# Latents normed in the input projection, latent products in split halves, and two gate units moved to the S5 stage

## The reference, cut to what matters

```python
proj = h @ w_in
c_q, c_kv, k_r, fq, fk, fv, f_logit, u, gate_logits = jnp.split(proj, split_points, axis=-1)
q  = einsum('bsr,rhd->bshd', rms_norm(c_q, q_lat_norm_g), w_uq)      # 384 -> 4 heads x 96
kv = einsum('bsr,rhd->bshd', rms_norm(c_kv, kv_lat_norm_g), w_ukv)   # 256 -> 4 heads x 128
k_nope, v_mla = kv[..., :64], kv[..., 64:]
k_mla = concatenate([k_nope, k_rope], -1)       # k_rope = k_r for each head
q_mla = apply_rope_tail(rms_norm(q, mla_q_norm_g), cos, sin)
k_mla = apply_rope_tail(rms_norm(k_mla, mla_k_norm_g), cos, sin)
o_mla = causal_block_attention(q_mla, k_mla, v_mla)
...
gates = sigmoid(gate_logits.reshape(bsz, seq, 3, 1024))
merged = einsum('bsnd,bsnd->bsd', gates, projected)
```

## Time and profile before

| | |
|---|---|
| median of 3 runs | 1647.36 us (1645.93 to 1648.49) |
| profiled execution, its own time | 1651.23 us |
| its span, first to last instruction | 1649.4 us |
| TensorE busy | 1521.9 us, 92% |
| VectorE busy | 939.9 us, 57% |
| ScalarE busy | 621.7 us, 38% |
| GpSimd busy | 126.6 us, 8% |
| mean granted TensorE clock | 0.967 |

### The profile page before, as it was taken

One profiled execution on the slowest core, in us unless ns is written; L12 is line 12 of the kernel. 1 busy time (PEld: TensorE's weight loads), 2 busy tenths in 40 slices (PEclk: granted clock), 3 DMA queues, 4 the chain that ended last, 5 costly groups with the idle time before them and its releaser, 6 DMA issues. The chain is left out here.

```text
span 1649.4 us, 19066 instructions
## 1 busy us (share of the span) xinstructions
PE 1521.9 (92%) x7214; PEld 1265.8 (77%) x7214; DVE 939.9 (57%) x1290; ACT 621.7 (38%) x1013; POOL 126.6 (8%) x104
## 2 busy tenths in 40 slices
PE   5999999987997988787899978999999999999999
PEld 4899877776576777676678767888888888888887
DVE  4310345666285665674783557887778887433333
ACT  4310224541222554212452335555555555332322
POOL 1000150002033000310120100000000000000000
PEclk9899999997998999898999989999999999999999
DMA  5130131103022000313455112322222221644643
GB/s 193 44 121 1 47 94 34 38 27 130 19 83 66 31 26 26 90 48 113 156 190 215 54 39 64 102 77 90 77 77 90 90 77 68 212 148 145 245 143 138
DMA packets 126500, 153.65 MB, mean 93 GB/s; under 512 B 11530, under 2 KB 94397, under 8 KB 126141
## 3 DMA queue, kind: packets, MB, share of 16 engines
q1 hardware_dynamic: 126224, 152.40, 28.3%
q10 hardware_dynamic: 189, 0.08, 0.0%
HBM read 115.55 MB, written 36.31 MB: 92 GB/s over the span
## 5 line engine op out<-in xcount | busy, mean ns | idle before, releaser
L486 PE MATMUL ps<-split_arena 128*128 128x512 f32 x1152 | 298.9, 414 | 25.3 <-ACT plain_arena L521 8.6
L1715 PE MATMUL ps<-split_arena 128*128 128x512 f32 x1320 | 308.0, 390 | 4.7 <-DVE split_arena L2253 3.5
L1715 PEld LDWEIGHTS ps<-split_arena 128*128 128x128 f32 x1320 | 247.8, 188 | 57.2 <-DVE split_arena L2253 4.0
L486 PEld LDWEIGHTS ps<-split_arena 128*128 128x128 f32 x1152 | 221.9, 198 | 74.1 <-issue 21.3
L1805 PE MATMUL ps<-down_w,down_a 128*128 128x512 f32 x352 | 137.3, 390 | 0.7 <-DVE down_w L1782 0.7
L1807 PE MATMUL ps<-down_w,down_a 128*128 128x512 f32 x352 | 137.1, 390 | 0.0
L1806 PE MATMUL ps<-down_w,down_a 128*128 128x512 f32 x352 | 137.1, 390 | 0.0
L1778 DVE TENSOR_TENSOR down_a<-plain_arena,down_a 128x1024 fp32r<-128x1024 f32 x44 | 53.9, 1225 | 144.5 <-ACT down_a L1767 144.5
L1715 PE MATMUL ps<-up_b,split_arena 128*128 128x512 f32 x528 | 130.7, 398 | 5.0 <-DVE split_arena L1643 4.9
L1715 PEld LDWEIGHTS ps<-up_b,split_arena 128*128 128x128 f32 x528 | 101.7, 193 | 27.1 <-DVE split_arena L1643 5.2
L1767 ACT ACTIVATE down_a<-plain_arena 128x1024 fp32r<-128x1024 f32 x44 | 46.7, 1061 | 161.6 <-PE ps L1807 146.5
(11 more groups left out here) (333 smaller groups left out, 2495.5 us busy)
## 6 DMA issues: line engine op xcount, KB each, us to landing
plain_arena<-scr_act SPq DMA_DIRECT2D x44, 512.0 KB, 3.6
plain_arena<-in_w_in SPq DMA_DIRECT2D x24, 512.0 KB, 4.2
scr_gate<-plain_arena SPq DMA_DIRECT2D x48, 256.0 KB, 2.0
plain_arena<-scr_gate SPq DMA_DIRECT2D x24, 512.0 KB, 4.6
plain_arena<-in_w_up SPq DMA_DIRECT2D x22, 512.0 KB, 5.1
up_raw<-in_w_up SPq DMA_DIRECT2D x22, 512.0 KB, 5.1
scr_act<-plain_arena SPq DMA_DIRECT2D x22, 512.0 KB, 2.6
plain_arena<-in_w_down SPq DMA_DIRECT2D x44, 256.0 KB, 3.9
```

The lines of the kernel that those rows point to most:

```text
L486: mm = nc.tensor.matmul(m.ps[:, self.banks[half], :], w[:, k, :], src[:, k, h * BANK:(h + 1) * BANK], start=(j == 0), stop=(j == self.PER_ ...
L1715: mm = nc.tensor.matmul(o, self.w[j][w][:, k, :], self.h[j][k][h], start=(j in self.OPENS and k == 0 and n == 0), stop=(k == self.HK - 1 a ...
```

## The change

It has six parts.

1. **Input projection.** ScalarE squares and sums the latents row tile by row tile (`lat_squares`, two row tiles behind the copies of chunk 1), VectorE makes the means, GpSimd the powers, VectorE scales the latents in place during chunk 3. The spill to memory waits for that.
2. **Latent transposes.** They need no norm any more and stand behind one gate unit instead of two. Each fill is split: ScalarE writes the high half with the gain, VectorE the low half. The two weights are split too, by ScalarE behind the sixth fill and by VectorE behind the eighth. Half a gate unit stands between the transposes and the products.
3. **Products.** Three fp32r matmuls each in place of one float32 matmul.
4. **Preparation of q and k.** ScalarE copies k's part; VectorE does square, sum and mean of k and of q first, then the low halves of v, then the rest. GpSimd's order is two splits of gate weights, the two powers, and then all other splits.
5. **The queue.** The 35 loads for S5 stand behind the units of the preparation; the semaphores of the stages before are cleared in the MLA stage, ahead of its last unit.
6. **Gate units.** 4, 1, 4, 4, 3 in place of 4, 2, 5, 3, 2: two units move from the MLA stage to the S5 stage, one to each of its groups.

Several buffers move within the core's memory; the squares of the preparation lie in another arena.

```diff
# stage_load_norm_project
-            sp.wait_ge(out_act, copied(2 * TT - 2))
-            sp.wait_ge(out_dve, copied(2 * TT - 1))
+            sp.wait_ge(lat_normed, 2 * TT)
             sp.dma_start(m.scr_lat, m.lat.rearrange("p a b -> p (a b)")).then_inc(spill, 16)
...
+            m.pool_step(nc.gpsimd.memset(lat_expo, -0.5))
+            pool.wait_ge(lat_ms, 2 * TT)
+            nc.gpsimd.tensor_tensor(lat_rstd, lat_ssq, lat_expo, ALU.pow).then_inc(lat_rstd_done, 1)
...
+            def lat_squares(t):
+                act.wait_ge((out_act, out_dve)[t % 2], copied(TT + t))
+                for i, (a, b) in enumerate(lat_parts):
...
+                    nc.scalar.activation(cols(m.R, 30720, b - a), m.lat[:, t, a:b], ACT.Square,
+                                         accum_out=lat_ssq[:, i * TT + t:i * TT + t + 1]).then_inc(lat_sq, 1)
...
+                if 0 <= n - TT - 2 < TT:
+                    lat_squares(n - TT - 2)
...
+                if n == 2 * TT + 3:
+                    dve.wait_ge(lat_sq, 2 * TT)
...
+                if 0 <= n - 2 * TT - 5 < 4:
+                    dve.wait_ge(lat_rstd_done, 1)
...
-FOX_PREP, MLA_FIRST, MLA_PREP, S5_FIRST, S5_SECOND = 4, 2, 5, 3, 2
+FOX_PREP, MLA_FIRST, MLA_PREP, S5_FIRST, S5_SECOND = 4, 1, 4, 4, 3
# stage_mla, SyncE
+            fill.sync(sp, MLA_FIRST + MLA_PREP)
             for i, v in enumerate((m.ins["s5_lambda_re"], m.ins["s5_lambda_im"])):
...
-            fill.sync(sp, MLA_UNITS)
+            fill.sync(sp, H - 1)
+            for x in past:
+                sp.sem_clear(x)
+            fill.sync(sp, 1)
# GpSimd
-            fill.gpsimd(pool, 1)
-            for n, (a, b) in enumerate(((0, 16), (16, 48), (16, 48))):
+            fill.gpsimd(pool, 2)
+            for n in range(2):
                 pool.wait_ge(ms_done, n + 1)
...
+            fill.gpsimd(pool, MLA_UNITS - 2)
# ScalarE
             for f in range(10):
                 act.wait_ge(filled, f + 1)
...
+                if f == 5:
+                    act.wait_ge(w_in, 48)
+                    for hi, raw in zip(w_hi, w_raw):
+                        nc.scalar.activation(hi, raw, ACT.Copy).then_inc(w_hi_done, 1)
+            fill.scalar(act, UNIT // 2)
...
+            nc.scalar.activation(k[:, :, :, 0:NOPE], kv[:, :, :, 0:NOPE], ACT.Copy).then_inc(k_out, 1)
# TensorE
-            fill.tensor(pe, UNIT)
+            fill.tensor(pe, MLA_FIRST * UNIT)
...
-            fill.tensor(pe, (MLA_FIRST - 1) * UNIT)
-            pe.wait_ge(scaled, 2)
+            pe.wait_ge(lat_in, 16)
+            for f in range(10):
+                r, half = divmod(f, 2)
+                if f >= 4:
+                    pe.wait_ge(lat_lo_done, f - 3)
...
+            fill.tensor(pe, UNIT // 2)
+            pe.wait_ge(lat_lo_done, 10)
+            pe.wait_ge(w_lo_done, 3)
+            def product(o, r, w, row, t, first, last):
+                cut = slice(t * P, (t + 1) * P)
+                for n, (x, y) in enumerate(((lat_hi[:, r, cut], w_hi[w]), (lat_hi[:, r, cut], w_lo[w]), (lat_lo[r][:, cut], w_hi[w]))):
+                    mm = nc.tensor.matmul(o, x, y[:, row, :], start=(first and n == 0), stop=(last and n == 2))
...
-            fill.tensor(pe, MLA_PREP * UNIT)
+            fill.tensor(pe, MLA_PREP * UNIT - UNIT // 2)
# VectorE
+            for f in range(10):
+                dve.wait_ge(lat_hi_done, f + 1)
+                V.scalar_tensor_tensor(out=lat_lo[f // 2][:, lat_cut(f)], in0=m.ps[:, f % 4, :], scalar=lat_gain(f),
...
+                if f == 7:
+                    for i in range(3):
+                        dve.wait_ge(w_hi_done, i + 1)
+                        V.tensor_tensor(w_lo[i], w_raw[i], f32(w_hi[i]), ALU.subtract).then_inc(w_lo_done, 1)
...
+            for n in range(2):
+                step(V.tensor_tensor(sq, flat[n], flat[n], ALU.mult))
+                step(V.tensor_reduce(ssq[n], sq, AX.X, ALU.add))
+                V.tensor_scalar(ssq[n], ssq[n], 1.0 / QK, EPS, ALU.mult, ALU.add).then_inc(ms_done, 1)
             for h in range(H):
                 dve.wait_ge(v_hi, h + 1)
...
             for n, (a, g) in enumerate(((k, gk), (q, gq))):
...
+                dve.wait_ge(rstd_done, n + 1)
```

## The result

The changed kernel took **1621.94 us** (median of four runs, 1620.49 to 1622.98), the kernel before 1646.64 us beside it (1645.64 to 1648.49): a ratio of 0.9844, 95% interval 0.9831 to 0.9856, 24.7 us less. The forecast was 1625.3 us. The profiled execution took 1622.98 us, with a span of 1621.3.

A forecast was written before the change was run, and what follows sets the result against it. TensorE, busy 92% of the span, bounds the kernel. Terms -9.4 - 5.1 - 14.5 + 7.1 = -22.0 us take the profiled 1651.23 to 1629.2; 3.9 us lower gives the median forecast, 1625.3 us, range 1615 to 1637.

The forecast's parts named there:

- Part 1: Input projection: the latents' squares, powers and scalings hide behind TensorE's work, at zero cost.
- Part 2: Latent stage up to the products: products start at 413.5 us, 9.4 us earlier, bounds 411.5 to 416.
- Part 3: Latent products: they take 23.8 us, where they took 28.9 us before.
- The "5 us" of cheaper products: Latent products: the share of the forecast gain put down to cheaper matmuls, 5.1 us in the sum.
- Part 4: From the products' end (P) to attention: attention starts at P + 50.1 = 487.4 us, 29.1 us earlier.
- the wait that takes the old one's place: Before attention: TensorE idles 8.9 us until GpSimd's gate split, made after the second power, ends at P + 25.5.
- three hits on VectorE: Between products and attention: three GpSimd gate splits lengthen VectorE's chain by 2.1 us each, to P + 48.9.
- Part 5: Attention: the 35 S5 loads (some 18 us of issue) and semaphore clears (11 us) cost zero there.
- Part 6: S5 stage: two more gate units lengthen it by 7.1 us, bounds +4 and +22.
- The clock term: S5 stage: products behind the second VectorE wait no longer run at clock 0.50, about 3 us back.
- The rule on the shared port: Before attention: by it both powers would hold VectorE's chain, some 10 us more; the forecast applied it to gate splits only.

The follow-up runs named there:

- e7: The changed kernel without the norm of the latents (no squares, mean, power or scaling in the input projection): ratio 0.9849.
- e6: The kernel before with one edit, the 35 S5 loads issued behind the last unit ahead of attention: ratio 1.0016.
- e11: The kernel before with one edit, the norm of the latents moved into the input projection: ratio 1.0013.
- e12: The kernel before with two edits, the latents' norm in the input projection and the S5 loads issued late: ratio 0.9954.
- e9: The changed kernel with latent products as before, one matmul each on whole FP32 operands, no low halves of latents and weights: ratio 0.9885.
- e1: The changed kernel with no gate unit moved to S5, and three GpSimd splits in place of two ahead of the powers: ratio 0.9947.
- e3: The changed kernel with the gate-weight split that TensorE waits for made ahead of GpSimd's two powers: 1618.48 us, ratio 0.9821.
- e10: The changed kernel with q's square on ScalarE, q taken first, and the gate-weight split TensorE waits for between GpSimd's two powers: 1614.91 us, ratio 0.9797.
- e4: The changed kernel with each of GpSimd's two powers of 32 values computed twice, one behind the other: ratio 0.9902.

## Why the prediction was right, step by step

It was right in the total within 3.4 us, in part by luck, since two of its terms were off by 4.0 and 3.1 us in opposite directions. Against S, the forecast had the products at 30.2 us, attention at 104.1 and 22.0 us off S to C; measured are 26.2, 103.0 and 24.4.

- **Part 1, the norm hides: right** (e7: nothing to gain by leaving it out).
- **Part 2, products at 413.5: 4.0 us too late**, and outside the bounds of 411.5 to 416. I charged 2.1 us for a GpSimd split on VectorE's path and 1 us for a fallen clock on TensorE's. Neither came. The split ran from 407.76 to 410.66, and the two low halves of fills inside it, with one input in PSUM, took 0.70 us each like the others (0.75 in the earlier trace rows); TensorE's granted clock was 1.00 throughout (row below). Each path was shorter besides: the transposes ended at 403.5 and not at 406.8, since the last fill waits only for the sixth low half (ready at 403.05), and the tenth low half was ready at 409.76, where I had 411.2 ahead of the charge. I had also treated two waits as one: removing the copy-out's wait alone, or the norm's alone, brings nothing (e6, e11), and both bring the 8 us (e12). The forecast counted both as removed, so its number stood, but a reader who had kept one of the two edits by my text would have gained nothing.
- **Part 3, products at 23.8 us: right** (23.6). The "5 us" of cheaper products in my sum leave out what making the halves costs ahead of them, 2.1 us (e9); that cost lay unnamed in part 2.
- **Part 4, P + 50.1: 3.1 us too short** (53.2). The step that failed is "GpSimd makes that only after the second power (P + 17.5 + 5.4 = P + 23.0) and in 2.4 us: P + 25.5". GpSimd's rows of the changed kernel, then the two of VectorE that lie across them:

```profile
443.41 8.48 POOL L1079 TENSOR_TENSOR statb<-stat,plain_arena 128x32 f32<-128x32 f32 x1 [32.74 <-DVE stat L1181]
451.86 5.67 POOL L1079 TENSOR_TENSOR stat<-stat,plain_arena 128x32 f32<-128x32 f32 x1
457.50 4.46 POOL L556 TENSOR_TENSOR split_arena<-plain_arena,split_arena 128x1024 fp32r<-128x1024 f32 x1
```

```profile
443.24 3.35 DVE L1179 TENSOR_TENSOR mla_sq<-plain_arena 128x3072 f32<-128x3072 f32 x1
...
456.40 3.36 DVE L1190 TENSOR_TENSOR plain_arena<-mla_sq,rowg 128x3072 f32<-128x3072 f32 x1
```

The first power is 3.05 us longer than 5.43, since the square of q (443.24 to 446.59) was under way; the split is 2.1 us longer than the 2.38 of the earlier trace rows, since VectorE's product with the gain ran until 459.76. Not all of the 3.05 us counts: q's sums were ready only at 450.20 (P + 16.8, where I had 17.5), so the second power began 1.7 us late, and took 0.2 more. With the split's 2.1 us, and less the 0.7 that the sums were early, the split ended at P + 28.5 and not P + 25.5. Everything else of this part stood: the wait that takes the old one's place, who ends it, the 24.6 us of two units behind it (24.6 measured), three hits on VectorE, whose chain ended at P + 48.1 (forecast 48.9).
- **Part 5, attention absorbs loads and clears: right** (146.4 against 146.5 us). SyncE issues them from 491.36 on, and its next load follows without anybody waiting:

```profile
492.83 9.03 SPq L1064 DMA_DIRECT2D vecs<-in_s_c_re  x16
...
509.30 0.42 SPq L487 DMA_DIRECT2D plain_arena<-in_w_in  x1
```

- **Part 6, S5 +7.1: 1.3 us too much** (+5.85 against before). By units, against e1: first +4.0 where I had 5.0; second +2.1 to 2.9 where I had 5.0 less 3 for the clock. The clock term held: the granted clock behind the second group is 1.00 (737 to 742 us), where it was 0.50.

In the sum against S: -4.0 (part 2), -0.2, +3.1 (part 4), -0.1, -1.3 (part 6) is -2.5 us of the 3.4 between 1625.3 and 1621.9; the rest is within the spread of the runs.

**Where the gain sits.** e12 and e1 make a second sum. The kernel before with norm and loads moved has S to C of 392.1; the changed kernel without the two moved units, which has besides them the halves, the statistics first and a half unit ahead of the products, has 392.2. So these three together bring nothing: TensorE's idle time between S and A is 8.2 us in e12 (1.65 + 0.81 + 5.48 + 0.29) and 12.8 us in e1 (0.34 + 0.56 + 11.87). The halves alone bring 3.2 us in the trace (e9), and the wait of 11.9 us is there with and without them; so what takes back their gain is most likely the new order of the preparation, with the split behind both powers. No run has that order by itself in the kernel before, so this is argued and not shown; e3 and e10, which change the order again, gain 6.6 and 8.8 us of S to C. The moved units bring 14.4 us. They do not fill idle time of the latent stage, which stays at 12.8 us (0.33 + 0.57 + 11.86 in the changed kernel): they leave it, and S5 takes part of them into its own idle and slow time. Norm and loads 10.1, units 14.4, together 24.5 us in the traces; 7.6 and 17 us by the ratios. Whether the two units could have been moved in the old order was not tried.

**The rule on the shared port.** The trace bears it out by halves. A split holds VectorE (5.42 us against 3.36), VectorE holds a power or a split until its own instruction ends (8.48 against 5.43; 4.46 against 2.4), and a power does not hold VectorE (3.36 us inside it). The Trainium skill, "SBUF — State Buffer" (section "SBUF: two separate sides"), lets whichever starts first keep the pair for its whole instruction. I had used it in one direction alone; taken in the other as well, with the terms of part 4, it would have given about P + 53 to P + 54 for attention's start (an estimate) and not P + 50.

## What to carry to other kernels

When the profile names what ended a wait, work out when the next condition on the same engine's path would have been met: if it lies within a microsecond or two, neither edit pays alone, and they must be made together. When two engines share a port, price both directions, and look at which short instruction of the queue in front of the bottleneck starts inside a long one of the other engine; moving one split ahead of two powers brought a seventh of what the whole change brought, by the ratios, and over a quarter by S to C. Work that can stand anywhere belongs where the bottleneck engine waits for another: a unit costs 10.6 to 10.8 us in the latent stage, whose wait it does not fill, and 2 to 4 us in the S5 stage, whose waits it does.

## What the runs showed of the hardware that I had not expected

- GpSimd's power of 32 values (5.4 us) lets VectorE run full products of two inputs inside it at their 3.36 us, yet one that begins while such a product is under way ends late by about what is left of the product (8.48 us with 3.2 left, 6.70 with 1.4 left). A product that is under way when the power ends does not lengthen it (5.42 us, e4's third).
- TensorE's granted clock stayed at 1.00 through transposes that followed dense matmuls. In the same view as the earlier trace rows: e12 has 40 FP32 transposes straight behind dense gate matmuls, e6 the same 40 behind 6.93 us of idle time. The windows (stretch, us, busy us of PE, PEld, DVE, ACT, POOL, granted clock, DMA share, GB/s), e12 first, then e6, then the transposes and half unit of the changed kernel:

```profile
408.55:415.10 6.55, 4.92 (x41) 4.23 (x39) 0.00 (x0) 5.89 (x10) 0.00 (x0) 1.00 0.00 1
```

```profile
415.39:423.50 8.11, 6.63 (x40) 6.39 (x40) 0.14 (x1) 6.32 (x10) 0.00 (x0) 0.74 0.00 0
```

```profile
397.40:409.80 12.40, 11.49 (x66) 8.74 (x65) 9.46 (x15) 9.48 (x15) 2.04 (x1) 1.00 0.07 25
```

At 2.4 GHz throughout the transposes take 4.92 us; behind the idle time, at a mean of 0.74, they take 6.63. In e6 that mean hides a rise: from 413 to 419.4 us the granted clock was 0.50, and from 420.4 on it was 1.00, while TensorE had done nothing but transposes since 415.39:

```profile
418.40:419.40 1.00, 1.00 (x7) 1.00 (x6) 0.00 (x0) 0.83 (x2) 0.00 (x0) 0.50 0.00 0
...
420.40:421.40 1.00, 1.00 (x11) 1.00 (x10) 0.00 (x0) 1.00 (x3) 0.00 (x0) 1.00 0.00 0
```

The Trainium skill, "TensorE: Matmul & The Clock Gate" (section "Part 4: PE-mode transpose"), says that a transpose does not count as busy for the clock in the way a matmul does. These traces do not bear that out: behind matmuls no fall of the clock shows in 5 to 6 us of transposes, and in e6 the clock rose during them.
